# Attention head order in a two-layer encoder: score products grouped by key/value head instead of alternating between the two

## What is computed

```python
qb = q.reshape(B, nb, BLOCK, N_KV_HEADS, G, HEAD_DIM)        # nb blocks of 128 tokens, G = 4, HEAD_DIM = 64
kw, vw = band(k), band(v)                                    # previous, own and next block
s = einsum('bnqhgd,bnkhd->bnhgqk', qb, kw) / sqrt(HEAD_DIM)
s = where(|k - q| <= 128 and k inside the sequence, s, NEG)
m = maximum(max(s), sink)
p = exp(s - m)
denom = sum(p) + exp(sink - m)
o = einsum('bnhgqk,bnkhd->bnqhgd', p / denom, vw)
```

## Time and profile before

| | |
|---|---|
| median of three runs | 2328.09 us |
| the profiled execution's own time | 2328.09 us |
| its span (first to last instruction) | 2326.4 us |
| mean granted TensorE clock | 0.967 |
| PE busy | 2177.5 us, 94% of the span |
| DVE busy | 1320.5 us, 57% |
| ACT busy | 992.8 us, 43% |
| attention slots, layer 0 | from 94.1 to about 301 us |
| attention slots, layer 1 | from 1217.4 to about 1424 us |

### The profile page before, as it was taken

How to read it: one execution, slowest core, us unless ns; L and a number is a source line. 1 busy time by engine, 2 the same in 40 slices (tenths; PEclk the granted TensorE clock), 3 DMA queues, 4 the chain that set the end, 5 groups by cost and what they waited for, 6 DMA issues and landing times.

```text
span 2326.4 us, 35484 instructions
## 1 busy us (share of the span) xinstructions
PE 2177.5 (94%) x13296; PEld 1830.2 (79%) x13296; DVE 1320.5 (57%) x2102; ACT 992.8 (43%) x1649; POOL 196.2 (8%) x236
## 2 busy tenths in 40 slices
PE   8899988999999899999788999899999989999998
PEld 7778957989889677777687886598988877777774
DVE  2775476533244766666767746835314466666667
ACT  2355565123332255555235547612323224555553
POOL 0000011000000331000200001100000022200004
PEclk9899989999999899999899999899999989999999
DMA  4045111232100599999511112123211038999996
GB/s 156 37 157 192 37 73 56 73 109 73 56 26 35 193 377 374 380 378 363 209 55 37 37 37 92 38 73 104 78 37 55 37 148 322 376 379 375 379 379 237
DMA packets 78548, 385.64 MB, mean 166 GB/s; under 512 B 10472, under 2 KB 11864, under 8 KB 43608
## 3 DMA queue, kind: packets, MB, share of 16 engines
q1 hardware_dynamic: 55264, 327.83, 37.6%
q0 software_dynamic: 10096, 30.38, 3.6%
q10 hardware_dynamic: 13064, 25.75, 3.0%
HBM read 352.79 MB, written 46.07 MB: 171 GB/s over the span
## 4 chain that ended last, share of the span: by engine, by line
PE 77%; DVE 12%; ACT 7%; issue 2%; DMA 1%; DVEq 0%; POOL 0%; ACTq 0%; SPq 0%; POOLq 0%
PE bank L2116 37%; PE bank L2593 10%; PE bank L2567 9%; PE bank L2557 8%; PE bank L2448 2%; DVE weight_slots_parts L1380 2%; PE bank L2132 2%; PE bank L2402 1%; PE bank L2533 1%; ACT x_transposed L1062 1%; PE bank L2285 1%; ACT weight_slots_parts L914 1%; PE bank L2256 1%; ACT scratch L1018 1%; DVE scratch L1532 1%
## 5 line engine op out<-in xcount | busy, mean ns | idle before, releaser
L2116 PE MATMUL bank<-weight_slots_parts,x_transposed_parts 128*128 128x256 f32 x2496 | 466.6, 289 | 4.5 <-ACT mixer_region L965 2.8
L2116 PEld LDWEIGHTS bank<-weight_slots_parts,x_transposed_parts 128*128 128x128 f32 x2496 | 397.0, 196 | 5.5 <-ACT mixer_region L965 3.2
L1824 DVE TENSOR_TENSOR weight_slots_parts<-weight_slots,mixer_region_parts 128x2048 fp32r<-128x2048 f32 x140 | 321.3, 2314 | 85.9 <-ACT mixer_region_parts L1207 85.8
L1207 ACT ACTIVATE mixer_region_parts<-weight_slots 128x2048 fp32r<-128x2048 f32 x140 | 261.0, 1909 | 23.7 <-ACT x_transposed L1282 18.1
L2116 PE MATMUL bank<-x_transposed_parts,weight_slots_parts 128*128 128x512 f32 (+1 forms) x1024 | 266.5, 348 | 1.8 <-DVE mixer_region L1489 1.8
L1380 DVE TENSOR_TENSOR weight_slots_parts<-weight_slots,weight_slots_parts 128x2048 fp32r<-128x2048 f32 x58 | 132.9, 2292 | 223.5 <-ACT weight_slots_parts L914 223.0
L2593 PE MATMUL bank<-weight_slots,x_transposed 128*128 128x512 f32 x560 | 246.4, 593 | 0.0
L2567 PE MATMUL bank<-mixer_region_parts,x_transposed_parts 128*128 128x256 f32 x1120 | 207.3, 283 | 0.4 <-DVE weight_slots_parts L1824 0.4
L2116 PEld LDWEIGHTS bank<-x_transposed_parts,weight_slots_parts 128*128 128x128 f32 x1024 | 183.4, 196 | 24.4 <-DVE mixer_region L1489 3.3
L2557 PE MATMUL bank<-mixer_region_parts,x_transposed_parts 128*128 128x512 f32 x560 | 193.0, 416 | 5.6 <-DVE x_transposed_parts L1829 5.6
L2593 PEld LDWEIGHTS bank<-weight_slots,x_transposed 128*128 128x128 f32 x560 | 103.4, 190 | 117.9 <-issue 101.7
(11 more groups left out here) (311 smaller groups left out, 3565.7 us busy)
## 6 DMA issues: line engine op xcount, KB each, us to landing
weight_slots<-in_w_gate SPq DMA_DIRECT2D x70, 1024.0 KB, 7.3
weight_slots<-in_w_up SPq DMA_DIRECT2D x70, 1024.0 KB, 7.1
weight_slots<-in_w_down SPq DMA_DIRECT2D x70, 1024.0 KB, 7.6
weight_slots<-in_w_in SPq DMA_DIRECT2D x20, 1024.0 KB, 5.0
slots_y<-x_transposed ACTq DMA_DIRECT2D x66, 256.0 KB, 7.2
weight_slots<-in_wkv_mem SPq DMA_DIRECT2D x16, 1024.0 KB, 4.9
slots_y<-in_consts SPq DMA_DIRECT2D x6, 2304.0 KB, 18.1
weight_slots<-in_w_out SPq DMA_DIRECT2D x8, 1024.0 KB, 5.1
```

Of the source, the lines that this page charges most:

```text
L1207: nc.scalar.activation(hi, raw, ACT.Copy).then_inc(moe.high_ready, 1)
L1824: v.tensor_tensor(lo, raw, hi.bitcast(F32), ALU.subtract).then_inc(moe.low_ready, 1)
L2116: ins = pe.matmul(ps, lhs[i](k), rhs[j](k), start=k == 0 and a == 0, stop=k == ks - 1 and a == 2)
```

## The change

A slot no longer takes two heads of each key/value head. It takes the four heads of one key/value head: slot 2c has n = 0 of block c, slot 2c + 1 has n = 1. `head_at` is gone. The probability tiles, sums, sinks and output columns of a slot follow the new order, which makes the sink row and the output columns of a slot contiguous.

```diff
-GROUP_ORDER = [(c, jp) for c in range(NC) for jp in range(GRP // 2)]
+GROUP_ORDER = [(c, n) for c in range(NC) for n in range(NKV)]
...
-def head_at(jp, t):
-
-    return t % NKV, 2 * jp + t // NKV
...
 (DVE)
-                            sk = sink[:, :].rearrange("p (n j) -> p j n", n=NKV)[:, 2 * jp:2 * jp + 2, :]
-                            top = st[:, 0:4].rearrange("p (j n) -> p j n", n=NKV)
-                            step(v.tensor_tensor(top, top, sk, ALU.max))
+                            sk = sink[:, n * GRP:(n + 1) * GRP]
+                            step(v.tensor_tensor(st[:, 0:4], st[:, 0:4], sk, ALU.max))
...
-                            step_ = v.tensor_tensor(y[:, c, 0:ATT].rearrange("p (n j d) -> p n j d", n=NKV, j=GRP)[:, :, 2 * jp:2 * jp + 2, :],
+                            step_ = v.tensor_tensor(y[:, c, n * 256:(n + 1) * 256].rearrange("p (j d) -> p j d", j=GRP),
...
 (PE)
-                            for t in range(GRP):
-                                n, j = head_at(jp, t)
-                                hp = slice(n * HD, (n + 1) * HD)
-                                key = ("sc", i, t)
+                            hp = slice(n * HD, (n + 1) * HD)
+                            for j in range(GRP):
+                                key = ("sc", i, j)
                                 ps = take(key)
                                 done(pe.matmul(ps[:, 0:nb * P], qT[hp, j, c * P:(c + 1) * P], kT[hp, k0 * P:(k0 + nb) * P],
                                                start=True, stop=True), key)
...
-                            for t in range(GRP):
-                                n, _ = head_at(jp, t)
+                            for j in range(GRP):
                                 for k in range(nb):
-                                    ins = pe.matmul(ps[:, t * HD:(t + 1) * HD], ptb[:, t, k * P:(k + 1) * P],
+                                    ins = pe.matmul(ps[:, j * HD:(j + 1) * HD], ptb[:, j, k * P:(k + 1) * P],
                                                     kv[:, k0 + k, NKV * HD + n * HD:NKV * HD + (n + 1) * HD],
                                                     start=(k == 0), stop=(k == nb - 1))
```

More of the change, by code:

```diff
@@ L1522, in _ @@
                         if i < 12:
-                            c, jp = GROUP_ORDER[i]
+                            c, n = GROUP_ORDER[i]
                             _, nb, m0 = keys_of(c)
@@ L1538, in _ @@
                             step(v.tensor_reduce(st[:, 0:4], probs[:, :, 0:nk], AX.X, ALU.max))
-                            sk = sink[:, :].rearrange("p (n j) -> p j n", n=NKV)[:, 2 * jp:2 * jp + 2, :]
-                            top = st[:, 0:4].rearrange("p (j n) -> p j n", n=NKV)
-                            step(v.tensor_tensor(top, top, sk, ALU.max))
+                            sk = sink[:, n * GRP:(n + 1) * GRP]
+                            step(v.tensor_tensor(st[:, 0:4], st[:, 0:4], sk, ALU.max))
                             v.tensor_scalar(st[:, 4:8], st[:, 0:4], -1.0, None, ALU.mult)
-                            v.tensor_tensor(st[:, 12:16].rearrange("p (j n) -> p j n", n=NKV), sk, top,
-                                            ALU.subtract).then_inc(m_ready, 1)
+                            v.tensor_tensor(st[:, 12:16], sk, st[:, 0:4], ALU.subtract).then_inc(m_ready, 1)
                             own(m_ready)
@@ L1548, in _ @@
                         if i:
-                            c, jp = GROUP_ORDER[i - 1]
+                            c, n = GROUP_ORDER[i - 1]
                             key = ("pv", i - 1)
                             tile_filled(dve, key)
-                            step_ = v.tensor_tensor(y[:, c, 0:ATT].rearrange("p (n j d) -> p n j d", n=NKV, j=GRP)[:, :, 2 * jp:2 * jp + 2, :],
-                                                    bank_of(key)[:, 0:256].rearrange("p (j n d) -> p n j d", j=2, n=NKV),
-                                                    st[:, ro:ro + 4].rearrange("p (j n) -> p n j", n=NKV).unsqueeze(3)
-                                                    .broadcast_to([P, NKV, 2, HD]), ALU.mult)
+                            step_ = v.tensor_tensor(y[:, c, n * 256:(n + 1) * 256].rearrange("p (j d) -> p j d", j=GRP),
+                                                    bank_of(key)[:, 0:256].rearrange("p (j d) -> p j d", j=GRP),
+                                                    st[:, ro:ro + 4].unsqueeze(2).broadcast_to([P, GRP, HD]), ALU.mult)
                             step_.then_inc(drain_sem(key), 1)
```

## The result

The changed kernel took 2340.22 us (median of 4 runs, 2338.27 to 2345.24) against 2328.07 us before: 12.2 us slower. The ratio on record, over more runs than these four, is 1.0054 with a 95% interval of 1.0038 to 1.0069, which is 8.8 to 16.1 us. The forecast was 14.0 us, and a time of 2342.1.

The account below looks back on a forecast made before the run. PE, busy 94% of the span, was taken to bound the kernel. Score products add 12.0 us per layer, of which 7.0 passes the slack; two layers give 14.0, so 2328.09 + 14.0 = 2342.1 us, own range 2336 to 2348.

Parts of the forecast that it names:

- Pairs over two halves, and 4 more steps of 0.215 or 0.32 us over one half: Score products: records no longer run two at a time, 8 steps instead of 4, adding 0.86 or 1.28 us per slot.
- Slot 0: First attention slot: PE waits 0.92 us for DVE behind the scores; of 1.7 us added at half clock, 0.8 passes on.
- Slot 1: Third transpose: slack 3.14 us takes the 0.8 us passed on to it and its own 0.86, leaving 0.
- Slack above 0.32 us hides, slot by slot: Third transpose's wait for ACT: 0.32 us is turnaround, anything above hides added PE time; 7.00 us per layer remains.
- The wait of slot 1 at 2.6 us or less: Sign in the profile after: PE's wait at the third transpose shrinks to this from 3.46 us.
- The waits for L965 and L1497 move along: PE's other attention waits, 1.4 us for ACT and 0.8 us for DVE, hide nothing.
- The sign that failed: Prediction is wrong if stages the change does not touch move by more than some 2 us through their clock.
- Exposed loads: Rival, chance 0.03: score weight loads add to each step, 0.405 or 0.51 us; 22.2 us per layer, 2372 us.
- Nothing hidden: Rival, chance 0.08: ACT's slack is spent as its work comes later with the scores; all 24.0 us count, 2352 us.
- No effect on PE: Rival, chance 0.06: paired records are two passes of one 64-row score product, so order does not matter; 2328 us.
- Half the price: Rival, chance 0.08: a score product's second record still overlaps the next's first; 2.65 us per layer, 2333.4 us.
- The clock giving it back: Rival, chance 0.03: more gap-free PE work, then less half-clock time around slot 0 and in the mLSTM stage; 2313 us.

Follow-up runs that it names:

- the pair of doublings: Kernel before with the four score products issued twice, in slots 1, 2 and 3 or in slots 8 to 11: 2330.27 and 2335.72 us against 2328.97.
- the doubling in slots 1 to 3: Kernel before with the four score products issued a second time in slots 1, 2 and 3 of each layer: 2330.27 us against 2328.97, ratio 1.0005.

## Why the prediction was right

- *Pairs over two halves, and 4 more steps of 0.215 or 0.32 us over one half:* right. The records start one by one, and a slot of 256 columns is 0.86 us longer (16.96 against 16.11 from slot 8 to 9).
- *Slot 0:* 0.8 us was to pass on. In both layers the first streamed matmul stands 3.71 us behind the first score instead of 3.00: 0.71. *Slot 1* was to take all of it: from the first score of the layer to slot 1's third transpose it is 16.52 us in both kernels.
- *Slack above 0.32 us hides, slot by slot:* right to 0.1 us in layer 1, as the table shows, and by the pair of doublings, which put the same work in two places and paid 1.3 and 6.8 us.
- *The wait of slot 1 at 2.6 us or less:* only in one of the two layers, 2.72 and 2.30 us (3.46 and 3.57 before). The path to the third transpose has a fixed length, 16.52 us in every kernel of this case, and the printed wait is what PE's own work leaves of it; that depends on how much of the work ran at half clock (in layer 0, a granted clock of 0.77 over this path with the 2.72 us, and of 0.79 with 3.13 us in another execution of the changed kernel).
- *The waits for L965 and L1497 move along:* right, 1.4 and 0.8 us in both.
- *DVE costs nothing:* right, 424 ns for the output before and after.
- *14.0 us in all:* measured 12.2, 14.3 and 10.3 us in three sessions by the medians, intervals from 6.8 to 17.9. The stage in the traces says 12.9. From slot 2's first score to the first mLSTM product it is 181.0 to 181.5 us in the three traces of the changed kernel, and 174.0 in both layers before: 7.2 us a layer, 14.4 in all. The 1.5 us between 14.4 and 12.9 are the stretch ahead of it, from slot 1's third transpose to slot 2's scores, whose half-clock part the forecast took as fixed. It is 16.21 and 16.05 us in the one profile before, 15.1 to 16.1 in the changed kernel, and 15.0 to 15.8 in the three other kernels that issue slots 0 to 2 with the same number of steps as before. So the profile before was at the long end, and the runs do not part this difference from chance. It is within the 4 us that the forecast allowed for it.
- *The sign that failed.* The forecast called itself wrong if stages that the change does not touch moved by more than some 2 us. One did, the 808.3 us from the long row of products in layer 1 on, which became 816 to 818. As kernels without the change show up to 817.5 us there, single traces of this kernel are not steady enough for that sign.
- *The rivals.* Exposed loads: refuted by the loads under matmuls in the changed kernel. Nothing hidden: refuted by the shrunken waits and the doubling in slots 1 to 3. No effect on PE: refuted by the starts. Half the price: refuted by the starts too, as no two of the eight records over one half start together. The clock giving it back: the mLSTM stage behind, from the first mLSTM product to the long row of products, took 94.7 and 94.2 us before and 93.9 and 94.0 after, so nothing of that size.

## What to carry to other kernels

Two float32 matmuls that each use 64 of the array's partitions ran at once here when they were on different halves and not more than four records apart. Ordering heads so that a slot has only one half took the scores from 4 steps to 8 (1.13 us to 1.99, 1.56 to 2.84 with 384 columns), with no instruction added and nothing in the shapes of the profile's rows that tells of it. Before pricing more work on the busiest engine, read the next wait of that engine in each slot: what it exceeds the other engine's turnaround by is free, and only that. And where a turnaround wait stands beside independent work, put the work into it; here that was worth 0.73 us where 0.32 were printed. Read its price from the distance of starts, and look for the wait that the moved work used to cover.

## What the runs showed that I had not expected

- PE reaches past four records of one half (the one that starts and three that wait) to start a record of the other half beside it, and not past more: four pairs of starts with the order 0, 0, 1, 1, and twelve steps instead of eight with 0, 0, 0, 0, 1, 1, 1, 1 (2.96 us instead of 2.00 for 16 records).
- A wait printed as 0.32 us cost 0.73 us of a slot's 16.11, 0.48 of it at the wait itself and 0.14 at the next tile's, where no idle time is printed.
